# A two-layer decoder step on one core: routing from the raw residual with square sums beside it, norm scale and weight put on token and gathered parts, one low part placed earlier

## What is computed

```python
def rmsnorm(x, g):
    y = x * lax.rsqrt(jnp.mean(x * x, axis=-1, keepdims=True) + EPS)
    return y * g

def moe(x, router_w, wg, wu, wd):          # x is rmsnorm(residual, norm_ffn)
    logits = x @ router_w                  # 264 x 8
    top_v, top_i = lax.top_k(logits, 2)
    gates = softmax(top_v)
    out = sum over e: combine[:, e] * (silu(x @ wg[e]) * (x @ wu[e])) @ wd[e]

x = x + mem_attend(rmsnorm(x, norm_mem), mk, mv, w_mq, w_mo)
hn = rmsnorm(x, norm_ffn)
x = x + moe(hn, ...)                       # layer 1
```

## Time and profile before

| what | value |
|---|---|
| median of 3 runs | 1156.31 us (1155.24 to 1158.59) |
| the profiled execution | 1157.79 us, span 1155.6 us |
| PE matmul busy | 94% of the span |
| DVE busy | 68% |
| ACT busy | 56% |
| mean granted TensorE clock | 0.964 of 2.4 GHz |

### The profile page before, as it was taken

How to read it: one execution, slowest core, us unless ns; L and a number is a source line. 1 busy time by engine, 2 the same in 40 slices (tenths; PEclk the granted TensorE clock), 3 DMA queues, 4 the chain that set the end, 5 groups by cost and what they waited for, 6 DMA issues and landing times.

```text
span 1155.6 us, 19981 instructions
## 1 busy us (share of the span) xinstructions
PE 1081.2 (94%) x7722; PEld 1022.7 (88%) x7722; DVE 784.2 (68%) x1089; ACT 649.6 (56%) x881; POOL 21.4 (2%) x40
## 2 busy tenths in 40 slices
PE   5999988899999998998989888999999999999995
PEld 4999886799999998998976788999999999999984
DVE  5598643466655565589633447898889888888873
ACT  5676533455433444585423345776767676776761
POOL 0001000000000000002010000000000000000000
PEclk8999999899999998998999878999999999999997
DMA  8444567945555554543469444998989898988951
GB/s 343 154 157 140 165 250 282 358 159 185 181 184 181 183 182 140 166 147 125 159 239 360 167 175 151 351 334 311 363 288 359 295 358 298 359 288 324 342 207 40
DMA packets 64275, 272.99 MB, mean 236 GB/s; under 512 B 7328, under 2 KB 7584, under 8 KB 63552
## 3 DMA queue, kind: packets, MB, share of 16 engines
q1 hardware_dynamic: 62352, 264.33, 64.4%
q0 software_dynamic: 1408, 7.12, 1.7%
q10 hardware_dynamic: 432, 0.38, 0.1%
HBM read 265.83 MB, written 5.98 MB: 235 GB/s over the span
## 4 chain that ended last, share of the span: by engine, by line
PE 74%; DVE 12%; DMA 5%; ACT 5%; issue 2%; SPq 1%; DVEq 0%; ACTq 0%
PE bank L634 11%; PE bank L636 11%; PE bank L635 11%; PE bank L631 10%; PE bank L632 10%; PE bank L633 10%; DMA ring<-dense 5%; DVE wl L1451 3%; ACT wh L1065 2%; DVE rstd L1445 2%; PE bank L658 2%; DVE sq L1462 1%; PE bank L751 1%; PE bank L789 1%; PE bank L913 1%
## 5 line engine op out<-in xcount | busy, mean ns | idle before, releaser
L1451 DVE TENSOR_TENSOR wl<-ring,wh 128x1024 fp32r<-128x1024 f32 x170 | 207.0, 1224 | 190.1 <-ACT wh L1065 188.6
L631 PE MATMUL bank<-xh,wh 128*128 128x264 f32 x928 | 273.7, 295 | 24.2 <-DVE xl L1467 16.7
L1065 ACT ACTIVATE wh<-ring 128x1024 fp32r<-128x1024 f32 x170 | 178.9, 1056 | 171.6 <-PE bank L633 124.0
L1712 DVE TENSOR_TENSOR wl<-ring,wh 128x1408 fp32r<-128x1408 f32 x144 | 232.5, 1622 | 56.7 <-ACT wh L1314 56.2
L632 PE MATMUL bank<-xl,wh 128*128 128x264 f32 x928 | 269.4, 290 | 0.0
L633 PE MATMUL bank<-xh,wl 128*128 128x264 f32 x928 | 268.6, 289 | 0.0
L1314 ACT ACTIVATE wh<-ring 128x1408 fp32r<-128x1408 f32 x141 | 194.6, 1381 | 52.8 <-PE bank L636 51.4
L631 PEld LDWEIGHTS bank<-xh,wh 128*128 128x128 f32 x928 | 180.6, 195 | 31.7 <-issue 27.8
L635 PE MATMUL bank<-wh,xl 128*128 128x352 f32 (+4 forms) x560 | 184.7, 330 | 0.0
L632 PEld LDWEIGHTS bank<-xl,wh 128*128 128x128 f32 x928 | 181.2, 195 | 0.0
L633 PEld LDWEIGHTS bank<-xh,wl 128*128 128x128 f32 x928 | 180.5, 195 | 0.0
(11 more groups left out here) (241 smaller groups left out, 1746.6 us busy)
## 6 DMA issues: line engine op xcount, KB each, us to landing
ring<-experts SPq DMA_DIRECT2D x192, 704.0 KB, 6.0
ring<-dense SPq DMA_DIRECT2D x234, 512.0 KB, 3.8
o_k<-kv POOLq DMA_DIRECT2D x2, 1024.0 KB, 4.4
o_v<-kv POOLq DMA_DIRECT2D x2, 1024.0 KB, 7.4
x<-xT SPq DMA_DIRECT2D x2, 528.0 KB, 4.9
o_y<-sq SPq DMA_DIRECT2D x4, 264.0 KB, 2.1
gatew<-gate_w POOLq DMA_DIRECT2D x2, 512.0 KB, 8.2
mem<-memT SPq DMA_DIRECT2D x1, 1024.0 KB, 13.2
```

Source lines behind the costliest of these rows:

```text
L631: mm(out, s_hi, m_hi, start=start, stop=False)
L1065: A(parts(k)[0], raw(u), ACT.Copy).then_inc(hi_ready, 1)
L1451: V.tensor_tensor(w_lo, raw(u), w_hi.bitcast(F32), ALU.subtract)\
L1712: V.tensor_tensor(w_lo, eraw(jj % ESLOTS), w_hi.bitcast(F32), ALU.subtract)\
```

## The change

1. Layer 1's square sum and the logits become one group of bank use, `lq`: for each feature chunk, a product of the raw residual with the router weights times the norm's weights (`rwg`, 32 columns, output partitions 0 to 31), and one of the squares with 32 columns of ones (output partitions 32 to 63). ACT copies the 64 rows, PE turns them (`lt`, 3 transposes), and DVE has logits and sums by token.
2. The tokens are turned from raw `x`. Their scale is applied by ACT (`scale=token_rstd`) and DVE in the parts; the norm's weight is applied to the gathered parts, in eight pieces of 256 columns instead of four of 512. Top-2 is taken from raw logits, and their difference is scaled afterwards.
3. On ACT the tokens' high parts come ahead of `first_highs`; a root of one column is put ahead of the squares, so that its table is loaded there. On DVE the selection matrix is one instruction; four of the six low parts of tokens come behind it; the low parts of units 1 to 3 come behind the gathered ones; the other blocks' ranks come later.
4. PE waits for each gathered bank before the first products that read it, instead of all four.
5. In both layers DVE makes the low part of unit `mo` 0 ahead of its copy of the sample's attention result.

```diff
@@ bank_plan
-            out += [("lg", l, t) for t in range(3)]
+            out += [("lq", l), ("lt", l)]
...
@@ class Splitter
-            def upto(self, k):
-                while self.at < min(k if k in first_mo else k + 1, NSPLIT):
+            def upto(self, k, more=1):
+                while self.at < min(k if k in first_mo else k + more, NSPLIT):
...
@@ tensor
-            pe.wait_ge(s_rw, 16)
-            nn = [tiles[("lg", l, t)] for t in range(3)]
-            bb = [take_bank(n) for n in nn]
+            pe.wait_ge(rwg_ready, 1)
+            n = tiles[("lq", l)]
+            b = take_bank(n)
             for kc in range(KC):
-                pe.wait_ge(xn_ready, KC * (3 * l + 2) + kc + 1)
-                for t, (t0, rows) in enumerate(TOK):
-                    i = mm(bb[t][0:rows, 0:NE], xn[:, kc, t0:t0 + rows], rw[:, kc, :], start=(kc == 0), stop=(kc == KC - 1))
...
+                pe.wait_ge(sq_ready, KC * (3 * l + 2) + kc + 1)
+                mm(b[0:32, 0:T], rwg[:, kc, :], x[:, kc, :], start=(kc == 0), stop=(kc == KC - 1))
+                i = mm(b[32:64, 0:T], ones[:, 0:32], sq[:, kc, :], start=(kc == 0), stop=(kc == KC - 1))
+            full(i, n)
...
+            n = tiles[("lt", l)]
+            b = take_bank(n)
+            pe.wait_ge(lgT_ready, 1)
+            for t, (t0, rows) in enumerate(TOK):
+                i = nc.tensor.transpose(b[0:rows, t * 64:(t + 1) * 64], lgT[0:64, t0:t0 + rows], ident[0:64, 0:64])
+            full(i, n)
...
-                    if g == 0 and side == 0:
-                        for x in GATHER:
-                            wait_read(pe, *before(x))
...
+                                if g == 0 and gi == 0 and side == 0 and kc % 2 == 0:
+                                    wait_read(pe, *before(f"X{kc // 2}"))
@@ scalar
+                if l % 2:
+                    A(small[:, 95:96], eps[:, 0:1], ACT.Sqrt)
...
-            first_highs(0)
+            n = tiles[("lq", l)]
+            wait_full(act, n)
+            A(lgT[0:64, :], bank(n)[0:64, 0:T], ACT.Copy).then_inc(lgT_ready, 1)
...
+            A(token_rms[:, 0:2], logits_sums[:, 0:2, 32], ACT.Sqrt, bias=eps[:, 0:1], scale=1.0 / D).then_inc(rms_ready, 1)
+            A(token_rms[0:TS, 2:3], logits_sums[0:TS, 2:3, 32], ACT.Sqrt, bias=eps[0:TS, 0:1], scale=1.0 / D).then_inc(rms_ready, 1)
             act.wait_ge(tail_zeroed, 2)
+            act.wait_ge(rstd_ready, 1)
...
-                    A(tokh[0:rows, t, hp * 512:(hp + 1) * 512], bank(n)[0:rows, :], ACT.Copy).then_inc(oh_ready, 1)
+                    A(tokh[0:rows, t, hp * 512:(hp + 1) * 512], bank(n)[0:rows, :], ACT.Copy, scale=token_rstd[0:rows, t:t + 1])\
+                        .then_inc(oh_ready, 1)
+            first_highs(0)
...
-                    A(xgh[:, 2 * x4:2 * x4 + 2, :, :].rearrange("p c b s -> p (c b s)"), bank(n)[:, :], ACT.Copy).then_inc(xgh_ready, 1)
+                    for c in range(2):
+                        A(xgh[:, 2 * x4 + c, :, :].rearrange("p b s -> p (b s)"), bank(n)[:, c * 2 * CAP:(c + 1) * 2 * CAP], ACT.Copy,
+                          scale=col("norm_ffn", DEPTH - 1, 2 * x4 + c)).then_inc(xgh_ready, 1)
@@ vector
+                if l % 2:
...
+                    link(V.memset(rwg, 0.0))
+                    step(V.tensor_tensor(rwg[:, :, 0:NE], rw[:, :, :], gains, ALU.mult))
+                    signal(rwg_ready)
...
+                S.upto(start("mo", l) + 1, 0)
                 n = tiles[("pvs", l)]
                 wait_full(dve, n)
                 read(V.tensor_copy(o8, bank(n)[:, 0:HD]), n)
...
-            invert(tiles[("ssq", 3 * l + 2)], 0)
-            for m in range(KC):
-                V.scalar_tensor_tensor(out=xn[:, m, :], in0=x[:, m, :], scalar=col("norm_ffn", l, m), in1=rstd[:, 0, :],
-                                       op0=ALU.mult, op1=ALU.mult).then_inc(xn_ready, 1)
...
+            dve.wait_ge(rms_ready, 2)
+            V.reciprocal(token_rstd, token_rms).then_inc(rstd_ready, 1)
...
-                for t in range(3):
-                    for side in range(2):
-                        i = V.tensor_scalar(gsel[:, t, side, :], iota, pcol[:, t, bass.ds(2 * p + side, 1)], None, ALU.is_equal)
-                i.then_inc(gsel_ready, 1)
+                slots = iota.unsqueeze(1).unsqueeze(1).broadcast_to([P, 3, 2, CAP])
+                places = pcol[:, :, bass.ds(2 * p, 2)].unsqueeze(3).broadcast_to([P, 3, 2, CAP])
+                V.tensor_tensor(gsel[:, :, :, :], slots, places, ALU.is_equal).then_inc(gsel_ready, 1)
...
             gather_matrix(0)
-            for j in range(1, NBUF):
-                elow(0, j)
-
+            for t in (1, 2):
+                for hp in range(2):
+                    token_low(t, hp)
+            elow(0, 0)
...
             gate_columns(0)
+            gathered_low(0, main.prologue)
+            for j in range(1, NBUF):
+                elow(0, j)
             run_pass(main)
```

More of the change, by code:

```diff
@@ L161, in bank_plan @@
         out += [("mo", l, m) for m in range(KC)]
-        out += [("ssq", 3 * l + 2)]
         if l % 2 == 0:
+            out += [("ssq", 3 * l + 2)]
             out += [("kf", l, u) for u in range(2)]
@@ L365, in trunk_kernel @@
         second = rt[:, 309:333].rearrange("p (t e) -> p t e", t=3)
+        logits_sums = rt[:, 360:480].rearrange("p (t v) -> p t v", t=3)
+        rank1 = rt[:, 480:504].rearrange("p (t e) -> p t e", t=3)
+        token_rms = rt[:, 504:507]
+        token_rstd = rt[:, 507:510]
+        lgT = rms[:, 0, :]
+        rwg = gatew[:, 1, 2:4, :].rearrange("p c n -> p (c n)").rearrange("p (k e) -> p k e", k=KC)
         gate2 = rt[:, 340:344].rearrange("p (b k) -> p b k", b=2)
@@ L436, in trunk_kernel @@
         pz_ready = sem("sample_probs_ready")
+        rwg_ready = sem("gained_router_ready")
+        lgT_ready = sem("logits_and_sums_copied")
+        sums_ready = sem("token_sums_ready")
+        rms_ready = sem("token_rms_ready")
+        rstd_ready = sem("token_rstd_ready")
         lmax_ready = sem("top_ready")
@@ L873, in _, with turn_tokens @@
             l = DEPTH - 1
-            pe.wait_ge(s_rw, 16)
-            nn = [tiles[("lg", l, t)] for t in range(3)]
-            bb = [take_bank(n) for n in nn]
+            pe.wait_ge(rwg_ready, 1)
+            n = tiles[("lq", l)]
+            b = take_bank(n)
             for kc in range(KC):
-                pe.wait_ge(xn_ready, KC * (3 * l + 2) + kc + 1)
-                for t, (t0, rows) in enumerate(TOK):
-                    i = mm(bb[t][0:rows, 0:NE], xn[:, kc, t0:t0 + rows], rw[:, kc, :], start=(kc == 0), stop=(kc == KC - 1))
-                    if kc == KC - 1:
-                        full(i, nn[t])
-            for t, (t0, rows) in enumerate(TOK):
+                pe.wait_ge(sq_ready, KC * (3 * l + 2) + kc + 1)
+                mm(b[0:32, 0:T], rwg[:, kc, :], x[:, kc, :], start=(kc == 0), stop=(kc == KC - 1))
+                i = mm(b[32:64, 0:T], ones[:, 0:32], sq[:, kc, :], start=(kc == 0), stop=(kc == KC - 1))
+            full(i, n)
+            def turn_tokens(t):
+                t0, rows = TOK[t]
                 for hp in range(2):
@@ L887, in _ @@
                     for c in range(4):
-                        i = nc.tensor.transpose(b[0:rows, c * P:(c + 1) * P], xn[:, 4 * hp + c, t0:t0 + rows], ident)
+                        i = nc.tensor.transpose(b[0:rows, c * P:(c + 1) * P], x[:, 4 * hp + c, t0:t0 + rows], ident)
                     full(i, n)
+            n = tiles[("lt", l)]
[4 more added lines that the diff above has]
+            full(i, n)
+            for t in range(3):
+                turn_tokens(t)
             n = tiles[("ps", l)]
@@ L1253, in _ @@
                         S.upto(behind("mo", l, m, 5, nxt + 3))
-                root(tiles[("ssq", 3 * l + 2)], T, 1.0 / D)
                 if l % 2 == 0:
+                    root(tiles[("ssq", 3 * l + 2)], T, 1.0 / D)
                     high_parts(between=nxt + 4)
@@ L1716, in _ @@
             l = DEPTH - 1
-            invert(tiles[("ssq", 3 * l + 2)], 0)
-            for m in range(KC):
-                V.scalar_tensor_tensor(out=xn[:, m, :], in0=x[:, m, :], scalar=col("norm_ffn", l, m), in1=rstd[:, 0, :],
-                                       op0=ALU.mult, op1=ALU.mult).then_inc(xn_ready, 1)
             dve.wait_ge(kv_written, 32 * DEPTH)
[L1722 to L1728, removed]
-            for t in range(3):
-                wait_read(dve, tiles[("lg", l, t)])
+            step(V.memset(rt[:, 0:480], 0.0))
+            link(V.memset(token_rms, 1.0))
+            n = tiles[("lt", l)]
+            wait_full(dve, n)
+            turned_sums = bank(n)[:, 0:192].rearrange("p (t v) -> p t v", t=3)
+            step(V.tensor_copy(logits_sums[:, 0:2, :], turned_sums[:, 0:2, 0:40]))
+            read(V.tensor_copy(logits_sums[0:TS, 2, :], turned_sums[0:TS, 2, 0:40]), n)
+            wait_read(dve, n)
+            signal(sums_ready)
+            lg = logits_sums[:, :, 0:NE]
             for t in range(3):
```

(45 more changed lines are left out.)

8 lines of the change are left out of this document (6 added, 2 removed).

## The result

| | kernel before | changed kernel |
|---|---|---|
| median, first comparison | 1156.17 us (1155.24 to 1158.59, 5 runs) | 1149.1 us (1147.34 to 1150.46, 5 runs) |
| ratio, 95% interval | | 0.9935 (0.9912 to 0.9958) |
| median, second comparison (run i) | 1156.96 us (23 runs) | 1151.68 us (12 runs) |
| ratio, 95% interval | | 0.9956 (0.9936 to 0.9976) |
| span of the profiled execution | 1155.6 us | 1145.5 us |

The change is 7.1 us faster in the first comparison and 5.3 us in the second; 6.2 was forecast. The profiled execution of the changed kernel happens to be the fastest of its five, so its span differs by 10.1 us.

A forecast was written before the change was run, and what follows sets the result against it. PE, busy 94% of the span, was taken as the bound, with layer 1's router chain delaying the experts. -9.5 us there and +3.3 for part 5 gave -6.2, so 1150.1 us from the median 1156.31; range 1146.3 to 1154.5.

The forecast's parts named there:

- Sums: Layer 1's router: 32 records in two column groups overlap fully, so +0 us, bounded by 0 and +3.6.
- the Trainium skill's packing figure: Router sums: 2.38 times for three column tiles, 0.79 of ideal; sums would take 4.5 us, +0.9, kernel 1151.0.
- Rival (b): Router sums: the two column groups run one after the other, +3.6 us, 1153.7; chance 0.12.
- Token scale: Router, from sums to token scale: copy, three transposes and DVE's small steps bring the scale to 678.7, counted from 676.07.
- Full clock through the transposes: Router: PE pauses only 0.6 us, so 24 token transposes take 2.6 to 2.9 us instead of 5.10.
- ACT as the chain: Before the gather: token parts 3.8 us, weights 5.2, identity 0.29 on ACT set the gather's start, 9.4 us earlier.
- Gather to experts: From gather to first expert units: DVE's low part sets unit 1's start, 700.1 against 709.65, -9.5 us.
- PE's gap after the first four chunks: Start of the experts: a sign that the forecast is right, a PE gap of 1.5 to 2 us.
- Rival (c): Expert start: units 1 to 3 late on DVE and ring, PE waits 1 us more at each, +3, 1153.1; chance 0.11.
- Part 5: End of attention, both layers: the sample's copy behind the low part delays `mo`, +1.65 us each, +3.3 together.
- Rival (a): End of attention: part 5 costs nothing, the delay is caught up, -9.5 us, 1146.8; chance 0.12.
- Rival (d): Router: sums run unoverlapped at 1.2 GHz, +9.7, and transposes pace ACT, +1.4; total +4.9 us, 1161.2; chance 0.05.

The follow-up runs named there:

- run i: The changed kernel as it is, timed again on another chip beside the kernel before: 1151.68 us, ratio 0.9956.
- run c: The changed kernel with all eight products of the router's column group issued first, then all eight of the square sum's: 1153.73 us, ratio 0.9967 to the kernel before.
- run f: The changed kernel with ACT's four weight units ahead of its copy of logits and sums: 1152.93 us, ratio 0.9981 to the kernel before.
- Run e: The kernel before with six useless fp32 matmuls in PE's pause between square sum and logits: 1151.05 us, ratio 0.9967 to the kernel before.
- Run d: The changed kernel without part 5, ACT's identity ahead of its copy, low parts of units 1 and 2 moved earlier: 1143.76 us, ratio 0.9893 to the kernel before.
- run b: The kernel before with part 5 alone added: 1159.29 us, ratio 1.0026 to the kernel before.
- run a: The changed kernel without part 5: 1146.15 us, ratio 0.9909 to the kernel before.
- run l: Kernel of run h without its useless matmuls before the final norm's sum: 1141.34 us, ratio 0.9868 to the kernel before.
- run h: Kernel of run d with useless matmuls before each attention output projection, the first gather and the final norm's sum: 1140.54 us, ratio 0.9885 to the kernel before.

## Why the prediction was right

*Sums.* Full overlap of two groups was taken, from the earlier trace rows. It cost nothing: records of the two groups start within 0.01 us of each other, every 0.22 us, and the bank is read at 675.88, 3.8 us after the start, as before. The 0.9 us that I had worked out from the Trainium skill's packing figure (TensorE: Matmul & The Clock Gate, "Measured speedup vs the span model") did not show. Rival (b) priced the loss of overlap at 3.6; run c measured 2.7.

*Token scale.* 678.7 was forecast from 676.07, and the scale was there at 678.3 with the sums read at 675.88, 0.2 us sooner. *Full clock through the transposes*: held, 2.84 us. The warning of the Trainium skill (TensorE: Matmul & The Clock Gate, "HAM oscillation") that pauses bring the low clock agrees with these traces: after 0.6 us of pause the clock stayed at 1.00, and after 2.7 us in run f it fell, 0.67 in 685 to 688. Run e shows that a pause is not needed for a fall.

*ACT as the chain.* The step that the forecast rested on. Tokens 3.5 us (3.8 forecast), weights 5.1, identity 0.3; PE waited for the identity, 5.96 us. The gather came 10.2 us earlier than before, 9.4 forecast; of the 0.8 us between them 0.4 were there by the token scale (678.3), and 0.3 lie in the token parts, which follow each other every 0.59 us and not 0.63. Run d, which moved the identity, shows what was next in line: DVE's token parts, 1.2 us ahead.

*Gather to experts.* -9.5 forecast at unit 1; measured 709.65 to 699.11, -10.5, of which 0.2 were there when the sums began; by the end of the span it is -10.1. PE's gap after the first four chunks was 1.4 us (1.5 to 2 forecast), and units 2 and 3 came without a wait. Rival (c) is out, the ring and DVE kept up.

*Part 5.* +3.3 forecast. The two stalls are 2.3 and 1.9 us against 0.14, 3.9 together; run b times it at 3.0 us, run a at 3.0 or 5.4. The term that was undersized is PE's share: the two transposes ran at 1.2 GHz in layer 0 (0.66 us for two, 0.41 before), and `mo` started 0.6 us after DVE's last small part (0.5 in layer 1), where 0.14 was the handover before. Rival (a), that it is free, fell.

The sum, -6.2, stands between the two comparisons, -7.1 and -5.3. Some luck is in how close it is: from the start of the sums to unit 1 the change won 10.3 us, 0.8 more than forecast, part 5 cost 3.9, 0.6 more, and the two errors cancel in part. Rival (d) did not come about: the clock was 1.00 during the sums. What no run takes apart is the router's gain itself: that it is the removed steps is read from the chain of waits; the runs price only its clock (e), the overlap (c) and the order on ACT (d, f).

What stays open: why a single execution of one kernel can be 4 to 9 us from its median here. In the two profiled executions the stretch from `mo` of layer 0 to `mo` of layer 1 differs by 3.3 us, in favour of the changed kernel, although layer 1's stall of part 5 (1.8 us more than before) lies in it and there is hardly any other edit. So the 10.1 us between the two profiled spans are not all the change's: -10.3 and +3.9 make -6.4. In part the clock differs there (0.68 against 0.86 in 450 to 460, 0.88 against 1.00 in 620 to 630); I did not test it.

## What to carry to other kernels

Before moving an instruction ahead on an engine, look at what it waits for: part 5 put a wait for a DMA ahead of three small instructions that had been hidden in it, and cost some 3 us in a change that gained 10 at the router. When steps leave the chain, the chain jumps to another engine, and the next gain is there (the identity behind four weight units). And count a pause of PE twice: once for itself, and once for the work behind it that then runs at half clock.

## What the runs showed of the hardware that I had not expected

The granted clock fell while PE was busy all the time: in run e it is 0.64 in 679 to 682, with 3.00 of 3.00 us busy, under fp32 products of 8 moving columns. Transposes of 128 columns and sums of 264 columns kept it at 1.00 in the changed kernel. That the logits of the kernel before were slow for their own shape too, beside the pause ahead of them, is my reading of this one trace; no run varies the shape alone.

Two column groups of 32 overlap completely when their matmuls alternate, two at the price of one (3.8 us for 32 records, as for the 16 of before). When they stand group after group, they still overlap by four records of each, so that a record of the later group starts (681.16) ahead of the last ones of the earlier group (681.83).

Filling pauses by useless matmuls raised the clock and won little of it in time. In run l the gather ran at full clock, and PE then waited 1.03 us for DVE at unit 1. In run h the output projection of layer 1 ran at full clock and the sums behind it came only 0.9 us sooner after its start (646.31 to 670.40, in d 646.92 to 671.89).
